# Attention: the order in which SyncE issues the second inverse sums and the next loads

## The chip, the cores and the metric

The kernel runs on one core of one Trainium2 chip. The metric is the device time of one execution in microseconds, given as a median of several runs. TensorE (PE) multiplies, VectorE (DVE) and ScalarE (ACT) do the elementwise work, GpSimd (POOL) adds masks here, and SyncE (SP) issues nearly all DMAs, in the order of its own program.

## What is computed

One layer of a decoder for 1024 tokens of width 1024: RMSNorm, one input projection, an RG-LRU branch and an attention branch of 8 heads (head size 128), gates, an output projection, and a mixture of 32 experts. Only the attention branch matters here:

```python
c = jnp.cumsum(log_f, axis=1).transpose(0, 2, 1)
for qb in range(S // Q_BLOCK):               # 8 query blocks of 128
    s = jnp.einsum('bqhd,bkhd->bhqk', q[:, lo:hi], k[:, :hi]) * scale
    s = s + c[:, :, lo:hi, None] - c[:, :, None, :hi]
    s = jnp.where(causal, s, -jnp.inf)
    p = jax.nn.softmax(s, axis=-1)
    outs.append(jnp.einsum('bhqk,bkhd->bqhd', p.astype(v.dtype), v[:, :hi]))
```

## The kernel before

The kernel is a row of stages with a barrier of all engines between them; attention is the sixth of nine. Every float32 product is made from three products of high and low parts.

**A head in the attention stage.** The stage takes the heads h0 to h7 one after another (`i` is the pair, `c` the head in it, so head 2i + c). Of each head it takes the query blocks 7 down to 0, and a tile is one query block with all of its keys, so the tiles get shorter: tile 0 has 1024 keys, tile 7 has 128. All engines run the same list of steps, one tile each: `scores` of tile n on PE (L1097), `bias` and minimum on DVE (L1186, which writes `least`), the exponential with its row sum on ACT (L1146), the reciprocal of the sum on DVE (L1183, into `inv`, two steps later), the transposes back (`turn`, L1106), the split in high and low (L1140, L1161), three steps later. The products with the values (`values`, L1121) come in two groups of four tiles, the first (g = 1, tiles 0 to 3) seven steps after tile 3 and the second (g = 0, tiles 4 to 7) seven steps after tile 7, so in steps 2 and 6 of the next head. Behind each group DVE multiplies the result by the inverse sums: `output`, L1170, which writes `at_o`. It waits for the PE product and for the inverse sums of this half.

**The way of the inverse sums.** `inv` holds them along partitions, and `at_o` needs them along the free axis, the same in all partitions. So SyncE writes 2 KB of them to DRAM (L1032, "the write"), waits until that has landed, and reads them back to all 128 partitions (L1035, 256 KB, "the broadcast"). This is `inverses(i, c, g)`. The first half can be written when tile 3 has its reciprocal, the second half when tile 7 has its own.

**What SyncE does for a head.** `head(i, c)` issues in this order: the first half's write, the wait for its landing and its broadcast; the store of the previous head's second half (L1027, 256 KB); the values of the next head (L951, two DMAs of 512 KB; they wait for the previous head's products); the queries and keys (L946, 2048 KB) and the bias (L947, 512 KB) of the head after the next, which wait until the last tile of this head has its scores; the second half's write, the wait for its landing, its broadcast; the store of this head's first half. All these DMAs are on one queue. The head buffers are double (`c`), and so are `inv_b` and `o_sb` (by half). The last two heads load no queries and keys, and the last no values.

Of the kernel before, what the change touches and what calls it, by code (L numbers as in the profile page):

```python
# [90 lines left out]
class Kernel:  # L91
# [721 lines left out]
    def branch_out(self, branch):  # L813

        nc, k_ = self.nc, self
# [25 lines left out]
        with nc.Block() as block:  # L841
            @block.sync
            def _(sp):
                if branch == 0:
                    for s, c in both:
                        sp.wait_ge(k_.sig_stored[s][c], 16 * (D // WB))
                else:
                    for k in range(4, KD):
                        for g in range(2):
                            sp.wait_ge(k_.o_stored[g], 16 * (k + 1))  # L850
                        sp.wait_ge(in_lo, k - 3)
                        sp.dma_start(stage[k % 4][:, :], k_.o_d[k]).then_inc(in_loaded[k % 4], 16)

                def gates(i):
                    for s, c in both:
                        sp.wait_ge(gated[s][c], i)
                        sp.dma_start(sg[s][c][:, :], k_.sig_d[branch, 4 * i + 2 * s + c]).then_inc(loaded[s][c], 16)
                with sp.Fori(0, n_pairs - 1) as i:
                    gates(i)
                    for s in range(2):  # L860
                        k_.load_block(sp, s, p0 + i + 1, k_.w_block(weights, WB * (2 + s) + 2 * WB * i))
                gates(n_pairs - 1)
                if branch == 0:

                    for c in range(2):
                        sp.wait_ge(k_.qk_stored[c], 16 * NH)
                        sp.wait_ge(k_.v_stored[c], 16 * NH // 2)
                    sp.wait_ge(k_.bias_stored, 16)
                    for c in range(2):
                        if c == 0:  # L870
                            k_.load_head_qk(sp, 0, c)
                        k_.load_head_v(sp, 0, c)
                for s in range(2):
                    k_.load_block(sp, s, p0 + n_pairs, k_.w_block(following, WB * s))

            @block.tensor
            def _(pe):
                with pe.Fori(0, n_pairs) as i:
                    for s, c in both:
                        if c == 0:  # L880
                            pe.wait_ge(k_.w_lo[s], p0 + i + 1)
                        pe.wait_ge(gated[s][c], i)
                        k_.product(pe, k_.ps[2 * s + c], s, c, in_lo if (s, c) == (0, 0) else None).then_inc((k_.w_first, k_.w_used)[c][s], 1)

            @block.scalar
            def _(act):
                for k in range(KD):
                    if branch == 1:
                        act.wait_ge(in_loaded[k % 4], 16 * (k // 4 + 1))
                    act.activation(k_.uh[:, k, :], source(k), ACT.Copy).then_inc(in_hi, 1)  # L890
                def mixed_high(i, s, c):
                    if branch == 1 and (i, s, c) != (n_pairs - 1, 1, 1):
                        n = 4 * i + 2 * s + c
                        act.wait_ge(gated[s][c], i + 1)
                        act.activation(k_.mix_h[:, n, :], k_.mix[:, n, :], ACT.Copy).then_inc(mix_hi, 1)
                for i in range(n_pairs):
                    k_.split_hi(act, 1, p0 + i)
                    for c in range(2):
                        mixed_high(i, 0, c)
                    k_.split_hi(act, 0, p0 + i + 1)  # L900
                    for c in range(2):
                        mixed_high(i, 1, c)

            @block.vector
            def _(dve):
                for k in range(KD):
                    dve.wait_ge(in_hi, k + 1)
                    dve.tensor_tensor(k_.ul[:, k, :], source(k), k_.uh[:, k, :].bitcast(F32),  # L908
                                      ALU.subtract).then_inc(in_lo, 1)
                def mixed_low(i, s, c):  # L910
                    if branch == 1 and (i, s, c) != (n_pairs - 1, 1, 1):
                        n = 4 * i + 2 * s + c
                        dve.wait_ge(mix_hi, n + 1)
                        dve.tensor_tensor(k_.mix_l[:, n, :], k_.mix[:, n, :], k_.mix_h[:, n, :].bitcast(F32),
                                          ALU.subtract).then_inc(mix_lo, 1)
                for i in range(n_pairs):
                    k_.split_lo(dve, 1, p0 + i)
                    for s, c in both:
                        dve.wait_ge((k_.w_first, k_.w_used)[c][s], p0 + i + 1)
                        dve.wait_ge(loaded[s][c], 16 * (i + 1))  # L920
                        mix = k_.mix[:, bass.ds(4 * i + 2 * s + c, 1), :].rearrange("p a t -> p (a t)")
                        if branch == 0:
                            dve.tensor_tensor(mix, k_.ps[2 * s + c][:, :], sg[s][c][:, :], ALU.mult)\
                                .then_inc(gated[s][c], 1)
                        else:
                            dve.tensor_tensor(sg[s][c][:, :], k_.ps[2 * s + c][:, :], sg[s][c][:, :], ALU.mult)\
                                .then_inc(own, 1)
                            dve.wait_ge(own, 4 * i + 2 * s + c + 1)
                            dve.tensor_tensor(mix, mix, sg[s][c][:, :], ALU.add).then_inc(gated[s][c], 1)
                        mixed_low(i, s, c)  # L930
                        if (s, c) == (0, 1):
                            k_.split_lo(dve, 0, p0 + i + 1)
# [11 lines left out]

    def load_head_qk(self, eng, i, c):
        eng.dma_start(self.at_qk[c][:, :, :].bitcast(F32), self.qk_d[2 * i + c]).then_inc(self.qk_in[c], 16)  # L946
        eng.dma_start(self.at_bias[c][:, :], self.bias_d[2 * i + c].partition_broadcast(P)).then_inc(self.bias_in[c], 16)  # L947

    def load_head_v(self, eng, i, c):
# [4 lines left out]
    def attention(self):  # L954
# [4 lines left out]
        nc, k_ = self.nc, self  # L959
# [49 lines left out]
        def later(engine, semaphore, count):  # L1009

            if type(count) is not int or count > 0:
                engine.wait_ge(semaphore, count)

        with nc.Block() as block:
            @block.sync
            def _(sp):
                def load_qk(i, c):
                    sp.wait_ge(least, tiles * i - tiles + NT * (c + 1))
                    k_.load_head_qk(sp, i, c)

                def load_v(i, c):
                    sp.wait_ge(pv_mm, 4 * i - 2 + 2 * c)
                    k_.load_head_v(sp, i, c)

                def store(i, c, g):
                    sp.wait_ge(o_out, 4 * i + 2 * c + 2 - g)
                    sp.dma_start(k_.o_d[2 * i + c][:, g * HALF:(g + 1) * HALF], o_sb[g][:, :]).then_inc(stored[g], 16)  # L1027

                def inverses(i, c, g):
                    sp.wait_ge(inverted, tiles * i + NT * c + 8 - 4 * g)  # L1030
                    rows = k_.inv_d[4 * i + 2 * c + g]
                    sp.dma_start(rows, inv[c][:, 4 * g:4 * g + 4]).then_inc(inv_stored[g], 16)  # L1032
                    sp.wait_ge(inv_stored[g], 16 * (2 * i + c + 1))
                    later(sp, o_out, 4 * i + 2 * c - g)
                    sp.dma_start(inv_b[g][:, :], rows.rearrange("p b -> (p b)").partition_broadcast(P)).then_inc(inv_in[g], 16)  # L1035

                def head(i, c, first=False, last=False):
                    inverses(i, c, 1)
                    if not first:
                        j, d = (i, 0) if c else (i - 1, 1)  # L1040
                        store(j, d, 0)
                        if not last or d == 1:
                            load_v(j + 1, d)
                    if not last:
                        load_qk(i + 1, c)
                    inverses(i, c, 0)
                    store(i, c, 1)

                k_.load_head_qk(sp, 0, 1)
                head(0, 0, first=True)  # L1050
                head(0, 1)
                for i in range(1, turns - 1):
                    for c in range(2):
                        head(i, c)
# [1075 lines left out]
```

## Time and profile before

| | us |
|---|---|
| median of 3 runs | 1828.74 |
| lowest and highest | 1824.96 and 1829.16 |
| the profiled execution, its own time | 1828.22 |
| its span, from the first to the last instruction | 1826.5 |
| PE busy in the span | 1703.8 (93%) |
| DVE busy | 1037.0 (57%) |
| ACT busy | 840.3 (46%) |

The span starts at 0; attention runs from about 801 to 968 us. In a timeline a line is: start, duration, engine, line, operation, out<-in with the tile's shape, count, and in brackets the idle time of the engine before it and what ended it. "SPq" is SyncE issuing; the duration there is the time of issuing, not of the transfer. Where a line "waited" for several things, the one that came last is named.

### The profile page before, as it was taken

To read this page: it belongs to the slowest core of one execution; us is meant where nothing else is said; L and a number is where in the kernel's file an instruction comes from. 1 tells how busy PE (TensorE), PEld (TensorE's weight loads), DVE (VectorE), ACT (ScalarE), POOL (GpSimd) and SP (SyncE) were. 2 spreads that over 40 slices of the span, in tenths; PEclk is the share of its full clock that TensorE was granted. 3 is DMA by queue.
4 is the path that set the end of the run, shared out by engine and by line. 5 is a ranking of instruction groups with operands and counts; after the bars stand their busy time and mean duration, and the time that the engine had idled before them with its cause. 6 is when DMAs were issued, how large, how long until landed. Compare 5 with 4: busy or idle time off the path is not lost. (4 is left out here: it accounts for less than half of the span.)

```text
span 1826.5 us, 22589 instructions
## 1 busy us (share of the span) xinstructions
PE 1703.8 (93%) x8515; PEld 1364.1 (75%) x8515; DVE 1037.0 (57%) x1125; ACT 840.3 (46%) x845; POOL 137.6 (8%) x187
## 2 busy tenths in 40 slices
PE   5999999999999998999888999969999999999991
PEld 4888888889987887878777888846667777777760
DVE  4353444432213313247665433769988888888886
ACT  5433334241122212036553111247777777878772
POOL 1000000000000000011110000110000000000005
PEclk9999999999999999999999999979999999999995
DMA  4343333323331223546655240379999999999977
GB/s 151 93 153 95 109 96 131 115 100 111 134 132 63 92 93 137 183 154 230 212 170 180 92 166 36 121 285 391 399 390 398 392 398 392 392 399 392 398 293 280
DMA packets 151686, 390.36 MB, mean 214 GB/s; under 512 B 14009, under 2 KB 73481, under 8 KB 147537
## 3 DMA queue, kind: packets, MB, share of 16 engines
q1 hardware_dynamic: 138368, 343.20, 51.0%
q0 software_dynamic: 8384, 29.63, 5.1%
q10 hardware_dynamic: 4880, 16.82, 2.3%
q8 instruction: 34, 0.56, 0.1%
q14 instruction: 20, 0.16, 0.0%
HBM read 322.15 MB, written 67.46 MB: 213 GB/s over the span
## 5 line engine op out<-in xcount | busy, mean ns | idle before, releaser
L1608 DVE TENSOR_TENSOR e_l<-e_raw,e_h 128x2048 fp32r<-128x2048 f32 x192 | 439.2, 2290 | 64.8 <-ACT e_h L1602 64.5
L1602 ACT ACTIVATE e_h<-e_raw 128x2048 fp32r<-128x2048 f32 x192 | 367.8, 1917 | 84.9 <-PE ps L1637 50.2
L199 PE MATMUL ps<-uh,w_h 128*128 128x512 f32 x1008 | 312.9, 392 | 11.9 <-DVE ul L908 9.7
L199 PE MATMUL ps<-ul,w_h 128*128 128x512 f32 x1008 | 312.1, 391 | 0.0
L199 PE MATMUL ps<-uh,w_l 128*128 128x512 f32 x1008 | 311.7, 391 | 0.0
L183 DVE TENSOR_TENSOR w_l<-w_raw,w_h 128x2048 fp32r<-128x2048 f32 x38 | 87.1, 2292 | 328.5 <-ACT w_h L179 328.5
L199 PEld LDWEIGHTS ps<-uh,w_h 128*128 128x128 f32 x1008 | 189.8, 189 | 52.8 <-issue 13.2
L199 PEld LDWEIGHTS ps<-ul,w_h 128*128 128x128 f32 x1008 | 190.2, 189 | 39.8
L199 PEld LDWEIGHTS ps<-uh,w_l 128*128 128x128 f32 x1008 | 190.2, 189 | 39.7
L1624 PE MATMUL ps<-e_h,e_xth 128*96 128x512 f32 x512 | 205.1, 401 | 6.3 <-DVE e_l L1608 3.0
L1624 PE MATMUL ps<-e_h,e_xtl 128*96 128x512 f32 x512 | 202.6, 396 | 0.0
L1624 PE MATMUL ps<-e_l,e_xth 128*96 128x512 f32 x512 | 201.9, 394 | 0.0
L179 ACT ACTIVATE w_h<-w_raw 128x2048 fp32r<-128x2048 f32 x38 | 72.7, 1914 | 167.6 <-DMA w_raw<-w_in 82.6
L1624 PEld LDWEIGHTS ps<-e_h,e_xth 128*96 128x96 f32 x512 | 83.0, 162 | 46.4 <-issue 7.3
L1624 PEld LDWEIGHTS ps<-e_h,e_xtl 128*96 128x96 f32 x512 | 83.1, 162 | 36.0
L1624 PEld LDWEIGHTS ps<-e_l,e_xth 128*96 128x96 f32 x512 | 83.4, 163 | 31.9
L1637 PE MATMUL ps<-e_h,e_hth 128*96 128x512 f32 x256 | 82.6, 404 | 2.1 <-DVE e_htl L1758 2.1
L1637 PE MATMUL ps<-e_l,e_hth 128*96 128x512 f32 x256 | 80.3, 395 | 0.0
L1637 PE MATMUL ps<-e_h,e_htl 128*96 128x512 f32 x256 | 80.2, 394 | 0.0
L1689 POOL DMA_INDIRECT e_xg<-xn_d,slots_i x30 | 41.3, 1378 | 474.2 <-PE ps L1700 474.2
L211 PE MATMUL ps<-w_h,uh 128*128 128x256 f32 x256 | 72.6, 284 | 0.9 <-PEq L164 0.9
L1097 PE MATMUL ps<-at_qk 128*128 128x512 f32 (+3 forms) x288 | 71.2, 378 | 2.3 <-PEq L164 2.0
(285 smaller groups left out, 2375.3 us busy)
## 6 DMA issues: line engine op xcount, KB each, us to landing
e_raw<-w_exp_gate SPq DMA_DIRECT2D x64, 1024.0 KB, 20.2
e_raw<-w_exp_up SPq DMA_DIRECT2D x64, 1024.0 KB, 20.1
e_raw<-w_exp_down SPq DMA_DIRECT2D x64, 1024.0 KB, 19.5
w_raw<-w_in SPq DMA_DIRECT2D x28, 1024.0 KB, 5.6
qk_d<-qk SPq DMA_DIRECT2D x16, 1024.0 KB, 4.2
at_qk<-qk_d SPq DMA_DIRECT2D x8, 2048.0 KB, 11.6
y_d<-e_y ACTq DMA_DIRECT2D x32, 384.0 KB, 6.5
y_d<-zeros POOLq DMA_DIRECT2D x22, 384.0 KB, 4.2
```

The lines of the kernel that those rows point to most:

```text
L179: act.activation(self.w_h[s][:, :, :], self.w_raw[s][:, :, :], ACT.Copy).then_inc(self.w_hi[s], 1)
L183: dve.tensor_tensor(self.w_l[s][:, :, :], self.w_raw[s][:, :, :], self.w_h[s][:, :, :].bitcast(F32), ALU.subtract).then_inc(self.w_lo[s], 1)
L199: mm = pe.matmul(ps[:, h * HALF:(h + 1) * HALF], w[:, k, :], u[:, k, h * HALF:(h + 1) * HALF], start=first, stop=last)
L211: mm = pe.matmul(ps, u[:, k, rows], w[s][:, k, :], start=first, stop=last)
L1097: mm = pe.matmul(k_.ps[n % 2][:, at:end], q, qk[c][:, part, at:end], start=first, stop=last)
L1602: act.activation(self.e_h[m % SPLIT][:, :, :], self.e_raw[slot][:, :, :], ACT.Copy).then_inc(self.e_hi[m % SPLIT], 1)
L1608: dve.tensor_tensor(self.e_l[slot][:, :, :], self.e_raw[slot][:, :, :], self.e_h[m % SPLIT][:, :, :].bitcast(F32), ALU.subtract).then_inc( ...
L1624: mm = pe.matmul(ps, x[:, k, :], w[:, k, :], start=first and first_piece, stop=last and last_piece)
L1637: mm = pe.matmul(ps[:, c * HALF:(c + 1) * HALF], x[:, at, :], w[:, 2 * k + c, :], start=first, stop=last)
L1689: pool.indirect_dma_start(out=xg[b][:, :], out_offset=None, in_=k_.xn_d, in_offset=bass.IndirectOffsetOnAxis(ap=slots, axis=0)).then_inc(g ...
```

## The change

In a head, SyncE now issues the queries and keys of the head after the next, then does the second half's inverse sums (write, wait, broadcast), and only then issues that head's bias and the next head's values. The bias is split off `load_head_qk` into a function of its own; the two other callers call both, one behind the other, as before. The waits stay with their functions: `load_v` still waits for the products of the head whose buffer it fills.

```diff
@@ branch_out @@
                         if c == 0:
                             k_.load_head_qk(sp, 0, c)
+                            k_.load_head_bias(sp, 0, c)
                         k_.load_head_v(sp, 0, c)
@@ load_head_qk @@
     def load_head_qk(self, eng, i, c):
         eng.dma_start(self.at_qk[c][:, :, :].bitcast(F32), self.qk_d[2 * i + c]).then_inc(self.qk_in[c], 16)
+
+    def load_head_bias(self, eng, i, c):
         eng.dma_start(self.at_bias[c][:, :], self.bias_d[2 * i + c].partition_broadcast(P)).then_inc(self.bias_in[c], 16)
@@ attention, head(i, c) @@
                     if not first:
                         j, d = (i, 0) if c else (i - 1, 1)
                         store(j, d, 0)
-                        if not last or d == 1:
-                            load_v(j + 1, d)
                     if not last:
                         load_qk(i + 1, c)
                     inverses(i, c, 0)
+                    if not last:
+                        k_.load_head_bias(sp, i + 1, c)
+                    if not first and (not last or d == 1):
+                        load_v(j + 1, d)
                     store(i, c, 1)
 
                 k_.load_head_qk(sp, 0, 1)
+                k_.load_head_bias(sp, 0, 1)
                 head(0, 0, first=True)
```

## Rows read from the trace of the kernel before

**Rows 1.** The page's first line.

```profile
span 1826.5 us, 22589 instructions
```

**Rows 2.** Waits, 798 to 970 us: who waited for whom; total, times, longest.

```profile
DVE at_o L1170 <- PE ps L1121: 25.5, 11, 3.7
...
DVE at_o L1170 <- DMA at_invb<-inv_d: 19.0, 5, 4.2
```

**Rows 3.** Timeline of DVE in attention: first tile of a head, and `at_o`.

```profile
816.24 1.22 DVE L1186 CUSTOM_DVE_ANT_0 at_s<-ps,at_bias 128x1024 f32<-128x1024 f32 x1
...
833.98 1.21 DVE L1186 CUSTOM_DVE_ANT_0 at_s<-ps,at_bias 128x1024 f32<-128x1024 f32 x1
...
852.01 1.05 DVE L1170 TENSOR_TENSOR at_o<-ps,at_invb 128x512 f32<-128x512 f32 x1 [3.60 <-DMA at_invb<-inv_d]
...
854.71 1.21 DVE L1186 CUSTOM_DVE_ANT_0 at_s<-ps,at_bias 128x1024 f32<-128x1024 f32 x1
...
861.96 1.09 DVE L1170 TENSOR_TENSOR at_o<-ps,at_invb 128x512 f32<-128x512 f32 x1 [2.54 <-PE ps L1121]
...
937.14 1.05 DVE L1170 TENSOR_TENSOR at_o<-ps,at_invb 128x512 f32<-128x512 f32 x1 [3.84 <-DMA at_invb<-inv_d]
...
939.84 1.21 DVE L1186 CUSTOM_DVE_ANT_0 at_s<-ps,at_bias 128x1024 f32<-128x1024 f32 x1
...
966.54 1.05 DVE L1170 TENSOR_TENSOR at_o<-ps,at_invb 128x512 f32<-128x512 f32 x1 [2.33 <-PE ps L1121]
```

**Rows 4.** Timeline of PE just behind the first of those waits.

```profile
853.71 0.55 PE L1106 MATMUL ps<-ident,at_s 128*128 128x128 f32 x3 [2.21 <-DVE at_ptl L1161]
```

**Rows 5.** Timeline of SyncE's queue in attention: what it issues, and when.

```profile
814.32 0.32 SPq L1035 DMA_DIRECT2D at_invb<-inv_d  x1
815.39 0.33 SPq L946 DMA_DIRECT2D at_qk<-qk_d  x1
...
826.30 0.32 SPq L1035 DMA_DIRECT2D at_invb<-inv_d  x1
...
832.39 0.32 SPq L1035 DMA_DIRECT2D at_invb<-inv_d  x1
...
833.23 1.39 SPq L951 DMA_DIRECT2D at_v<-v_d  x2
834.66 2.46 SPq L946 DMA_DIRECT2D at_qk<-qk_d  x1
...
837.64 0.43 SPq L1032 DMA_DIRECT2D inv_d<-at_inv  x1
848.64 0.32 SPq L1035 DMA_DIRECT2D at_invb<-inv_d  x1
...
854.17 0.32 SPq L1035 DMA_DIRECT2D at_invb<-inv_d  x1
...
917.26 0.32 SPq L1035 DMA_DIRECT2D at_invb<-inv_d  x1
...
931.79 0.32 SPq L1035 DMA_DIRECT2D at_invb<-inv_d  x1
...
938.11 0.32 SPq L1035 DMA_DIRECT2D at_invb<-inv_d  x1
...
946.66 0.33 SPq L1035 DMA_DIRECT2D at_invb<-inv_d  x1
```

**Rows 6.** Windows: busy time of the engines, PEclk, DMA share, GB/s.

```profile
905.00:910.00 5.00, 4.64 (x34) 4.00 (x34) 4.81 (x16) 4.67 (x13) 0.92 (x3) 1.00 0.93 388
...
896.00:911.00 15.00, 14.56 (x86) 12.42 (x86) 11.82 (x35) 9.64 (x23) 2.76 (x6) 1.00 0.79 280
911.00:917.00 6.00, 3.67 (x27) 3.05 (x26) 2.30 (x9) 1.74 (x5) 0.86 (x2) 1.00 0.38 88
```

**Rows 7.** From issue to landing: all 16 broadcasts (L1035); the values issued at 938.95.

```profile
DMA to landing us min/median/max: 3.2/3.8/5.5
...
DMA to landing us min/median/max: 5.7/6.3/6.9
```

## The prediction

> **What bounds the kernel now.** The span is 1826.5 us [rows 1], and every stage ends in a barrier, so a stage that is shorter by some us makes the whole shorter by as much; the change touches attention alone. I read first who waits for whom in it. DVE's `at_o` waits in 11 of its 16 cases for PE's product, 25.5 us together, which is the normal turn of a step. In the other 5 it waits for the broadcast of the inverse sums, 19.0 us together, at most 4.2 [rows 2]. DVE stands still there with PE ready: at 852.01 it comes off a wait of 3.60 us, and PE, which runs ahead for a while, then stands for 2.21 us for the low half that DVE owes it [rows 3, 4].
>
> The price of this is read from the starts of the heads on DVE. From h1's first tile (816.24) to h2's (833.98), no `at_o` waited for a broadcast, and the head took 17.74 us. From there to h7's first tile (939.84) it is 105.86 us for five heads, 21.17 each [rows 3]. Five undisturbed heads would take 88.7, so **17.2 us** are the most that lies in this wait (a part of it is lower clock later in the stage).
>
> Then I read why the broadcast is late, on SyncE's queue. I name two moments of head h: F(h), when SyncE issues the broadcast of the first half, and S(h), of the second half. Both are moments at which a write has just been seen to land. F(1) is 832.39, S(1) 848.64, F(2) 854.17, and so on to F(5) 917.26, S(5) 931.79, F(6) 938.11 and S(6) 946.66 [rows 5]. From F to S is the **long stretch**: broadcast, store, values, queries and keys, bias, write, 4098 KB together; 16.25 us in h1 and 14.53 in h5. From S to the next F is the **short stretch**: broadcast, store, write, 514 KB; 5.53 us behind h1. In the long one the write of 2 KB issued at 837.64 is seen landed at 848.64, 11 us later, because it is last in the queue behind 3.5 MB of loads [rows 5]. F(1) to F(6) is 105.72 us, 21.14 a head: SyncE's own chain has DVE's pace. It is a closed ring: SyncE waits for a landing, issues, waits for the next landing, and the loads stand in the same queue as the small writes. So what bounds these five heads is **the sum of all transfers of a head and of two waits for a landing**, not the second half's wait by itself. That is the point the forecast turns on.
>
> **The change part by part.** Removed from each long stretch of h1 to h5: the values (1024 KB) and the bias (512 KB); from that of h0 the bias, and from that of h6 the values. Added to the short stretch behind it: the same. Calls and bytes are the same in all, and no wait is added; the split of the bias from the queries and keys is at no cost, as both are issued in either order by the same engine. The two callers outside `head` keep their order.
>
> *What a long stretch loses (a).* The nearest row is h0's long stretch, which has neither store nor values: from 814.32 to 826.30, 11.98 us. Of these 0.23 are a later issue of queries and keys (1.07 us behind the broadcast, where 0.84 is SyncE's usual distance from broadcast to the next load) [rows 5]. The bias, 512 KB at the 388 GB/s of a full stretch [rows 6], is 1.35 us, and the missing store of 256 KB at the same rate 0.7. So a long stretch of the new order is 11.98 - 0.23 - 1.35 + 0.7 = 11.1 us. The long stretches of now have a mean of (105.72 - 5 x 5.53) / 5 = 15.6. That gives a = 4.5; against h1's own 16.25 it is 5.2. I take 4.8, between them.
>
> *What a short stretch gains (b).* The nearest row is the long stretch of h6, which has no queries, keys and bias: broadcast, store, values and write from 938.11 to 946.66, 8.55 us [rows 5]. Less the short stretch's 5.53, the values cost 3.0, and with 1.35 for the bias b is 4.4. At the mean rate of the stretch that is loading, 280 GB/s [rows 6], the 1536 KB take 5.6, the upper bound. I take 4.8, nearer to the first: the row has the very transfers, and the write there was not last behind a store, which makes it a little short. So a and b are equal, and **the ring stays as long as it is**.
>
> *The waits move.* In the new order S(h) comes 4.8 us sooner against F(h), and the next F is where it was. DVE needs 7.25 us from a head's first tile to the first half's `at_o` (854.71 to 861.96) [rows 3] and was ready for h1's second half at 852.01 - 3.60 = 848.4. S(1) falls from 848.64 to 843.8 and its broadcast lands 3.8 us later [rows 7], at 847.6: the first of the five waits is gone. Then DVE, at 17.74 a head, catches up with the ring of 21.1 again, and the rest of the waits come back smaller, and at the first half's `at_o` too, which now has the long queue ahead of it. The ring's pace is DVE's pace once more, only with DVE further ahead.
>
> *How far ahead at the end.* By S: S(5) = 931.79 - 4.8 = 927.0, landed at 930.8, and h7 begins 2.7 us later (852.01 to 854.71), at 933.5. From h7's first tile to the last `at_o` are 966.54 - 939.84 = 26.7 us [rows 3], which gives 960.2. By the ring: F(6) = 938.1 as before. h6 now has a long stretch without values: S(6) = 938.1 + 5.5 = 943.6. The values of h7 go behind it: F(7) = 943.6 + 8.55 = 952.2. Then S(7) = 952.2 + 5.5 = 957.7, and with 3.8 for the broadcast the last `at_o` starts at 961.5. The ring is later than DVE, so it decides: 961.5 instead of 966.54, **5.0 us less**. In the kernel before, the ring was no bound at this end, since DVE was far behind it. Here it takes back 1.3 us of what DVE has won.
>
> *The values are later.* They are issued behind the broadcast at S + 0.8 and landed up to 6.9 us after issue without a bias ahead [rows 7]; with it, some 8.2, so at S + 9.0. PE needs them about 2.4 us after the next head's first tile (4.6 us of products before the `at_o` at + 7.25), and that tile starts at S + 3.8 + 2.7 = S + 6.5: PE needs them at S + 8.9. That is a tie, and costs nothing as long as `at_o` needs the first half's broadcast, which lands at S + 10.3 + 3.8 = S + 14.1. The bias is needed a whole head later, and is covered.
>
> The Trainium skill's page "DMA: Bandwidth & Descriptors", section "Anatomy of one DMA — SWDGE (gpsimd) path", gives each DMA about 2.0 us fixed, most of it the receipt of the last write, and its bytes at 436 GB/s. By this the long stretch would be some 11.6 us and h6's 5.6; the trace has 15.6 and 8.55, so I don't go by it. By it alone the bytes moved behind the short stretch would partly fall into fixed time that is idle now, which is the first rival.
>
> **The rivals.** *The transfers hide in the short stretch.* From 911 to 917 the DMA engines are busy 0.38 of the time, at 88 GB/s, against 0.79 in the stretch before [rows 6]. 0.62 x 6 = 3.7 us stand idle, and if the bias and the values went into that, b would be 1.1 and not 4.8. Then the ring is 3.7 us shorter a head, 17.4, and DVE's own pace of 17.74 bounds: the waits vanish. Of the 17.2 us I leave some 2 to the lower clock: 15 less, 1813. Against it: h6's stretch, in which the values had the same idle time and still cost 3.0. A half-way case (b = 3.8) gives 5 us more than the forecast, 1818. Chance 0.16.
>
> *The wait only changes its place.* If b is larger than a by 0.8 to 1 us (a = 4.5 and b = 5.4, both inside their rows), each of the five heads loses 0.9, F(6) comes at 942.6, and the gain of 5.0 is used up: 1827.7. For it: in the short stretch the write stands right behind a store to DRAM. Chance 0.14.
>
> *Slower: PE waits for the values.* They were issued 10 us before the second half's broadcast and are issued behind it now. `at_o` of the second half needs the broadcast at S + 10.3 + 10.8 + 3.8 = S + 24.9 at the earliest, and from the values' landing to it are 4.9 + 7.3 = 12.2 us of work. So values that land later than S + 13 make every head longer, us for us. I have them at S + 9.0. SyncE can be held at issuing, too: queries and keys issued behind values took 2.46 us instead of 0.33 [rows 5], and the store and the next write now stand in that place. If they land at S + 15.5, five heads lose 2.5 each, 12.5, less the 5.0: 1836. Against it is the landing of 6.9. Chance 0.06. That the change doesn't do what it says can't be: SyncE issues in the program's order.
>
> **How the numbers follow.** Forecast: 1828.2 - 5.0 = **1823.2**, from the profiled execution's own 1828.22, which is 0.5 under the median of 1828.74. Each 0.5 us of difference between a and b is worth 2.5 us; with a from 4.5 to 5.2 and b from 4.4 to 5.6 the forecast's own range is 1819 to 1829. Chance 0.62; 0.02 is left for what I don't see. 0.3% is 5.5 us, about what a measurement of this kernel tells from no change; the forecast lies just inside it, so I give 0.26 of its 0.62 to faster and 0.36 to the same. Faster: 0.26 + 0.16 = 0.42. Same: 0.36 + 0.14 + 0.02 = 0.52. Slower: 0.06. The range reaches into the first rival: 1815.5 to 1829.2.
>
> **What would show it.** In the changed kernel's timeline of SyncE, from F to S about 11 us (10.4 to 11.1) and from S to the next F about 10.3, and their sum still near 21. If the sum falls below 20, the first rival is right; if it rises over 22, the second. DVE's waits for the broadcast should fall from 19.0 to between 8 and 13 us and be spread over more than five `at_o`, some of the first half. h3's first tile comes at 851.7 and not at 854.71. The last `at_o` starts near 961.5 and waits for its broadcast, and the write-to-landing time of the second half falls from 11 us to some 6. PE must show no long wait for `at_v`. The prediction is wrong if the ring's length depends on the order, that is, if a and b differ by more than 0.5.

## The result, and the profile after

The changed kernel takes 1829.75 us (median of 18 runs, 1826.4 to 1833.04), the kernel before beside it 1826.22 (18 runs, 1823.68 to 1829.16): 1.0016 times as long, 95% interval 1.0008 to 1.0023, so 1.5 to 4.2 us **slower**, where 5.0 us faster was forecast. By the bound of 0.3% it is no change; by its interval it is a small loss. The profiled execution took 1831.69 us.

The page's first line, then the waits from 798 to 975 us (who waited for whom: total, times, longest), answering to [rows 1, 2]:

```profile
span 1830.1 us, 22589 instructions
```

```profile
DVE at_o L1176 <- DMA at_invb<-inv_d: 26.5, 7, 4.6
...
POOL at_bias L1085 <- DMA at_bias<-bias_d: 21.6, 5, 5.8
DVE at_o L1176 <- PE ps L1127: 20.3, 9, 6.1
...
PE ps L1127 <- DMA at_v<-v_d: 1.9, 1, 1.9
```

DVE waits for broadcasts 7 times and not 5, 26.5 us and not 19.0. Where it does, the product of PE has become ready in the same time, so part of these waits was there before under PE's name. PE's wait for the values is small. All waits of `at_o` together are 46.8 us, where they were 44.5.

The timeline of DVE (start, duration, line, tile, and in brackets the idle time before it), answering to [rows 3]:

```profile
816.75 1.22 DVE L1192 CUSTOM_DVE_ANT_0 at_s<-ps,at_bias 128x1024 f32<-128x1024 f32 x1
...
852.23 1.21 DVE L1192 CUSTOM_DVE_ANT_0 at_s<-ps,at_bias 128x1024 f32<-128x1024 f32 x1
...
870.55 1.05 DVE L1176 TENSOR_TENSOR at_o<-ps,at_invb 128x512 f32<-128x512 f32 x1 [3.90 <-DMA at_invb<-inv_d]
...
881.75 1.10 DVE L1176 TENSOR_TENSOR at_o<-ps,at_invb 128x512 f32<-128x512 f32 x1 [3.41 <-DMA at_invb<-inv_d]
...
939.43 1.22 DVE L1192 CUSTOM_DVE_ANT_0 at_s<-ps,at_bias 128x1024 f32<-128x1024 f32 x1
...
968.78 1.05 DVE L1176 TENSOR_TENSOR at_o<-ps,at_invb 128x512 f32<-128x512 f32 x1 [2.31 <-PE ps L1127]
```

From h1's first tile to h3's are 35.48 us, twice 17.74: the first wait has gone, as forecast (36.05 in a second profile of the same kernel). Four heads later h7 begins 122.68 us after h1, where it was 123.60: nearly all of the start has been given back. To the last `at_o` are 152.03 us, against 150.30 before. Waits are now at the first half's `at_o` too (881.75). The 1.7 us between 152.03 and 150.30 are the part of the loss that attention shows in this pair of profiles. Of the 3.5 us between the two spans, 0.5 lie ahead of h1's first tile and 1.3 behind the last `at_o`, where both kernels issue the same in the same order. Two profiles of one and the same kernel differ by up to 2.2 us in these parts, so I can't place them.

The timeline of SyncE's queue, answering to [rows 5]; the broadcasts (L1038) are the moments F and S in turn:

```profile
833.32 0.32 SPq L1038 DMA_DIRECT2D at_invb<-inv_d  x1
833.68 0.44 SPq L1030 DMA_DIRECT2D o_d<-at_o  x1
834.16 0.43 SPq L947 DMA_DIRECT2D at_qk<-qk_d  x1
...
843.67 0.32 SPq L1038 DMA_DIRECT2D at_invb<-inv_d  x1
844.03 0.43 SPq L950 DMA_DIRECT2D at_bias<-bias_d  x1
844.51 1.25 SPq L954 DMA_DIRECT2D at_v<-v_d  x2
845.80 4.64 SPq L1030 DMA_DIRECT2D o_d<-at_o  x1
850.49 0.43 SPq L1035 DMA_DIRECT2D inv_d<-at_inv  x1
855.65 0.32 SPq L1038 DMA_DIRECT2D at_invb<-inv_d  x1
...
944.18 0.32 SPq L1038 DMA_DIRECT2D at_invb<-inv_d  x1
...
948.97 0.32 SPq L1038 DMA_DIRECT2D at_invb<-inv_d  x1
...
958.05 0.32 SPq L1038 DMA_DIRECT2D at_invb<-inv_d  x1
...
963.68 0.32 SPq L1038 DMA_DIRECT2D at_invb<-inv_d  x1
```

F(1) is 833.32, S(1) 843.67, F(2) 855.65, F(6) 944.18. The long stretches of h1 to h5 have a mean of 10.57 us (15.56 before), the short ones 11.61 (5.59 before). The ring F(1) to F(6) is **110.86 us** and was 105.72. So the long stretch lost 5.0 and the short one gained 6.0. The sum of the two, 22.2 us a head, is over the 22 that the prediction named as the sign of its second rival.

Windows of the same profile (busy time and number of instructions of PE, PEld, DVE, ACT, POOL; PEclk; DMA share; GB/s) at two of the waits:

```profile
870.00:872.00 2.00, 0.00 (x0) 0.00 (x0) 1.45 (x2) 0.00 (x0) 0.00 (x0) 0.94 0.97 286
872.00:875.00 3.00, 2.75 (x9) 2.46 (x10) 2.94 (x10) 1.49 (x4) 0.91 (x2) 0.50 1.14 320
...
936.00:938.00 2.00, 0.00 (x0) 0.00 (x0) 1.41 (x2) 0.00 (x0) 0.00 (x0) 1.00 0.87 238
938.00:941.00 3.00, 2.46 (x12) 1.90 (x13) 2.95 (x10) 1.18 (x4) 0.72 (x2) 1.00 1.15 327
```

PE does nothing from 870 to 872, and behind it the granted clock is 0.50, the lower of its two levels. Behind the like pause from 936 to 938 it stays at 1.00. A cost beyond the waits themselves isn't seen: h3 and h4 take 21.03 and 21.66 us from first tile to first tile, and 17.74 with the part of their waits that an undisturbed head doesn't have makes 21.22 and 21.74.

### The profile page after: what moved, and what is told of

Read it like the earlier page. It is cut to its first block and busy times, and to the rows that moved or that the text cites. A ratio compares the mean times of both kernels' runs of the same rounds, so it can differ in the third digit from the quotient of the medians.

```text
span 1830.1 us, 22589 instructions
## 1 busy us (share of the span) xinstructions
PE 1703.5 (93%) x8515; PEld 1362.6 (74%) x8515; DVE 1036.8 (57%) x1125; ACT 841.2 (46%) x845; POOL 138.5 (8%) x187
```

## The experiments

All are read by the same numbers: the means of the five long and the five short stretches of h1 to h5, the ring F(1) to F(6), the time from h1's first tile to the last `at_o`, and the ratio to the kernel before, run beside it, with its 95% interval. All in us but the ratio.

| kernel | long | short | ring | h1 to last `at_o` | median | ratio |
|---|---|---|---|---|---|---|
| before | 15.56 | 5.59 | 105.7 | 150.3 | 1826.22 | |
| before, second profile | 15.60 | 5.46 | 105.3 | 150.6 | | |
| changed | 10.57 | 11.61 | 110.9 | 152.0 | 1829.75 | 1.0016 [1.0008, 1.0023] |
| changed, second profile | 10.38 | 11.74 | 110.6 | 152.0 | | |
| e1, bias alone moved | 14.02 | 7.44 | 107.3 | 149.9 | 1830.84 | 1.0012 [1.0001, 1.0023] |
| e2, values alone moved | 11.83 | 10.07 | 109.5 | 150.8 | 1830.87 | 1.0010 [0.9999, 1.0021] |
| e3, changed, store first | 11.14 | 10.36 | 107.5 | 146.0 | 1827.25 | 0.9996 [0.9988, 1.0005] |
| e4, changed, bias behind values | 10.23 | 11.68 | 109.6 | 155.3 | 1834.08 | 1.0032 [1.0020, 1.0044] |
| e7, changed, values by head | 10.56 | 11.07 | 108.1 | 147.9 | 1824.51 | 0.9978 [0.9967, 0.9989] |
| e8, before, values by head | 14.69 | 5.71 | 102.0 | 143.0 | 1822.07 | 0.9965 [0.9953, 0.9978] |
| e10, before, no store ahead of the write | 15.71 | 4.41 | 100.6 | 141.8 | 1822.77 | 0.9975 [0.9964, 0.9986] |
| e5, loads in the landings | | | 89.2 | 132.8 | 1811.35 | 0.9910 [0.9895, 0.9924] |
| e6, inverse sums on GpSimd | | | | 139.8 | 1819.49 | 0.9949 [0.9936, 0.9963] |
| e9, e5 with values by head | | | 90.2 | 132.9 | 1810.76 | 0.9910 [0.9895, 0.9925] |

The kernel before beside e1 to e4 took 1828.57, beside e5 to e8 1828.25, beside the others 1827.80. The medians are of 4 to 12 runs, that of the changed kernel of 18, those of the kernel before of 16 to 29; each second profile is a single run (1827.12 and 1831.18 us). The stretches and the attention time are those of one profiled execution, which in e1 and e5 was the fastest of its kernel, so they and the medians need not agree to a us or two.

**Is the surplus of the ring real?** The two kernels once more, with no edit.

> The kernel before once more, for a second profile: how much of the differences between stretches is the spread from one execution to the next. If the ring is a property of the order, F(1) to F(6) is 105.7 within 1.5 us, the long stretch 15.6 and the short one 5.6 within 0.3.

> The changed kernel once more, for a second profile. If b is larger than a by a property of the order, F(1) to F(6) is 109 to 112, the short stretch 11.3 to 11.9 and the long one 10.3 to 10.9. If the 5 us between the two rings was chance, it comes out under 108.

Both rings come back within 0.5 us, and all four mean stretches within 0.2. The 5 us between the rings belong to the order and not to chance. In the second profile of the changed kernel the last `at_o` waits for its broadcast, as the forecast had it:

```profile
DVE at_o L1176 <- DMA at_invb<-inv_d: 38.5, 11, 4.8
```

**Which of the two moves makes it?**

```diff
 # e1: only the bias behind the second half's inverse sums
                         store(j, d, 0)
+                        if not last or d == 1:
+                            load_v(j + 1, d)
...
                         k_.load_head_bias(sp, i + 1, c)
-                    if not first and (not last or d == 1):
-                        load_v(j + 1, d)
 # e2: only the values
                         load_qk(i + 1, c)
+                        k_.load_head_bias(sp, i + 1, c)
                     inverses(i, c, 0)
-                    if not last:
-                        k_.load_head_bias(sp, i + 1, c)
```

> The bias alone is moved behind the second half's broadcast; the values stay ahead of queries and keys as in the kernel before. Measure: SyncE's ring from F(1) to F(6), 105.7 us before and 110.9 in the changed kernel, and the time. Theory A (the surplus comes from the values: SyncE is held 4 to 5 us at issuing the store behind them, so the store and the write start late): ring 105 to 107, time as before within 1.5 us. Theory B (the surplus comes from the bias, which is slow right behind the broadcast, both being spread to all partitions from one row of DRAM): ring 109 to 111, time 2 to 4 us above before.

> The values alone are moved behind the second half's broadcast; the bias stays with queries and keys. Theory A (hold at issue behind the values): ring F(1) to F(6) 109 to 111, SyncE's store issue still takes 4 us or more, time 2 to 4 us above before. Theory B (slow bias behind the broadcast): ring 105 to 107, time at or 1 to 4 us under before, because h6's stretch to S is shorter.

Moved alone, the bias takes 1.5 from the long stretch and gives 1.9 to the short one; the values take 3.7 and give 4.5. Both moves lose, 0.3 and 0.8 us a head, together the 1.1 of the change. e1's ring of 107.3 is just outside theory A, and far from theory B; e2's 109.5 is in theory A, but its store is issued in 2.1 to 3.9 us and not in 4 or more. The medians of both are 2.3 us over before though attention is at its old length. e1's interval just excludes no change and e2's doesn't, and the record doesn't say where these 2.3 us lie.

**The order behind the broadcast.**

```diff
 # e3
                     inverses(i, c, 0)
+                    store(i, c, 1)
                     if not last:
                         k_.load_head_bias(sp, i + 1, c)
                     if not first and (not last or d == 1):
                         load_v(j + 1, d)
-                    store(i, c, 1)
 # e4
                     inverses(i, c, 0)
+                    if not first and (not last or d == 1):
+                        load_v(j + 1, d)
                     if not last:
                         k_.load_head_bias(sp, i + 1, c)
-                    if not first and (not last or d == 1):
-                        load_v(j + 1, d)
                     store(i, c, 1)
```

> The changed kernel, but the store of the first half is issued right behind the second half's broadcast, ahead of bias and values. Theory A: the store's own latency is overlapped again, but the next write is now the one held behind the values; ring 107 to 110, so up to 0.7 us a head less than the 110.9 of the changed kernel. Theory B: with the store between broadcast and bias the bias is not slowed, ring 105 to 107.

> The changed kernel, but with the values ahead of the bias behind the second half's broadcast. Bytes and queue are the same. Theory A: SyncE is now held at issuing the bias, and the store and the write after it are late as before; ring 110 to 112. Theory B: the bias is no longer beside the broadcast, ring 106 to 107.5 and the time within 1.5 us of before.

e4 has the short stretch of the changed kernel, 11.68, and a ring of 109.6, just under theory A and far over theory B's 107.5: taking the bias away from beside the broadcast does not make the stretch shorter, and theory B falls. e4 shows something else on DVE's timeline, in front of h3's first tile:

```profile
855.09 0.16 DVE L1189 RECIPROCAL at_inv<-at_small 128x1 f32<-128x1 f32 x1 [2.45 <-POOL at_bias L1085]
855.17 1.22 DVE L1192 CUSTOM_DVE_ANT_0 at_s<-ps,at_bias 128x1024 f32<-128x1024 f32 x1
```

The head waits for its mask, and the mask for the bias: the bias of h3 is issued at S(1), in the middle of h2, and is needed 8.6 us later, not "a whole head later", as the prediction said; for h4 to h7 it is 7.0 to 7.5 us. In the changed kernel it has landed 6.3 to 6.7 us behind S, just in time (POOL waits 21.6 us for it; DVE's waits for POOL are 4.3 us together, as before). Behind the values it lands 9.4 to 11.8 us behind S, DVE waits 18.6 us for POOL, and attention is 3.3 us longer than in the changed kernel.

e3 is 1.25 shorter in the short stretch than the changed kernel and 0.6 longer in the long one; attention is 4.3 us shorter than before. Its median is not clear of before (0.9996, interval 0.9988 to 1.0005). The ring of 107.5 fits theory A in size, but the next two show that the hold is not the reason.

**Is SyncE held at issuing?** The store behind the values took 4.64 us to issue. A layout of the values in DRAM head by head makes runs of 4 KB out of runs of 512 bytes:

```diff
-        self.v_d = dram("v_d", (NH // 2, 2, P, NT, WB))
+        self.v_d = dram("v_d", (NH // 2, 2, P, 2, NT, HD))
...
-                          self.v_d[i, part, :, :, c * HD:(c + 1) * HD]).then_inc(self.v_in[c], 16)
+                          self.v_d[i, part, :, c, :, :]).then_inc(self.v_in[c], 16)
```

with the staging tiles of the stage that writes them in the same form.

> The changed kernel, with the values kept in DRAM head by head, so that a head's values are 2 x 128 runs of 4 KB instead of 2 x 1024 runs of 512 bytes. Theory A (SyncE is held at issuing behind the 2048 small runs, and store and write start late): the issue of the store behind the values falls from 4.2 us to under 1.5, the short stretch from 11.6 to 8.5 to 10 us, the ring F(1) to F(6) from 110.9 to 95 to 103, and the time by 4 to 12 us against the changed kernel. Rival (the bytes cost as much in either form): ring 108 or more.

> The kernel before, with the same head-by-head layout of the values in DRAM. Theory A: the issue of queries and keys behind the values falls from 2.5 to 0.5 us, the long stretch loses 1 to 2 us (15.6 to about 14), the ring falls from 105.7 to 97 to 102, time 4 to 8 us under before. Rival (bytes alone count): ring 104 to 106, time as before.

SyncE's queue in e7:

```profile
866.96 0.32 SPq L1038 DMA_DIRECT2D at_invb<-inv_d  x1
867.32 0.43 SPq L950 DMA_DIRECT2D at_bias<-bias_d  x1
867.80 1.03 SPq L954 DMA_DIRECT2D at_v<-v_d  x2
868.88 0.98 SPq L1030 DMA_DIRECT2D o_d<-at_o  x1
869.90 0.78 SPq L1035 DMA_DIRECT2D inv_d<-at_inv  x1
878.20 0.32 SPq L1038 DMA_DIRECT2D at_invb<-inv_d  x1
```

The hold is gone, 0.98 us where the same head of the changed kernel has 4.18, and the write is issued 2.9 us behind the broadcast where it was 6.4. But it is seen landed only 8.3 us later, where it was 4.2, and the short stretch has lost 0.54 in the mean. The layout takes 0.5 us off the stretch that has the values in the changed order and 0.9 off it in the order before; the surplus of the order stays: with this layout the short stretch gains 5.4 where the long one loses 4.1. So theory A of e7, that the hold makes the surplus, has fallen: its ring of 108.1 is in the rival's range. Its time is 5 us under the changed kernel, as theory A had it, but the layout gives as much in the old order. There, in e8, the numbers came as its theory A had them (ring 102.0, 6.2 us under before), but for the long stretch, which lost 0.9 and not 1 to 2. By the two ratios the layout is worth 6 to 7 us in either order.

**What does a store ahead of the write cost?**

```diff
                     if not first:
                         j, d = (i, 0) if c else (i - 1, 1)
+                        store(j, d, 1)
                         store(j, d, 0)
...
                     inverses(i, c, 0)
-                    store(i, c, 1)
+                    if last and c == 1:
+                        store(i, c, 1)
```

> The kernel before, with the store of a head's first half issued one long stretch later, so that nothing but the broadcast stands ahead of the next write. Theory receipt (a write that stands right behind a 256 KB store to DRAM is seen landed about 1 us later, beside the 0.7 us of the store's bytes): the short stretch falls from 5.6 to 3.8 to 4.2, the long one grows by 0.6 to 0.8, the ring F(1) to F(6) falls from 105.7 to 99 to 102, time 3 to 6 us under before. Rival (bytes alone count, so what the short stretch loses the long one gains): ring 105 to 106.5, time as before.

SyncE's queue there:

```profile
868.05 0.32 SPq L1035 DMA_DIRECT2D at_invb<-inv_d  x1
868.41 0.43 SPq L1032 DMA_DIRECT2D inv_d<-at_inv  x1
873.18 0.32 SPq L1035 DMA_DIRECT2D at_invb<-inv_d  x1
873.54 0.91 SPq L1027 DMA_DIRECT2D o_d<-at_o  x2
```

The short stretch falls from 5.5 to 4.4 in the mean (3.2 to 5.6 in the five heads; this one is one of the longer), and the long one grows by 0.1 only. So a 256 KB store right ahead of the small write costs 1.1 to 1.2 us, and in the middle of the long stretch next to nothing. This is what e3 has gained, 1.25. The theory had 0.7 us for the bytes in either place, and a short stretch of 4.2 at most; that was wrong, and the rest of it held: ring 100.6, attention 8.5 us shorter, the time 1.4 to 3.6 per mille less.

**Is the ring the bound?** The same transfers, with loads issued while a write is landing:

```diff
-                    inverses(i, c, 1)
+                    inverses_out(i, c, 1)
                     if not first:
                         j, d = (i, 0) if c else (i - 1, 1)
+                        if not last or d == 1:
+                            load_v(j + 1, d)
+                    inverses_in(i, c, 1)
+                    if not first:
                         store(j, d, 0)
                     if not last:
                         load_qk(i + 1, c)
-                    inverses(i, c, 0)
+                    inverses_out(i, c, 0)
                     if not last:
                         k_.load_head_bias(sp, i + 1, c)
-                    if not first and (not last or d == 1):
-                        load_v(j + 1, d)
+                    inverses_in(i, c, 0)
                     store(i, c, 1)
```

`inverses_out` is the first half of `inverses`, the write; `inverses_in` the wait for its landing and the broadcast.

> All transfers as in the changed kernel, but SyncE issues a load while each of its two writes is still landing: the next head's values between the first half's write and its broadcast, the bias between the second half's write and its broadcast. Theory ring (SyncE's chain of transfers and two waits for a landing is the pace of heads h1 to h6): the idle time of the landings, some 2 x 2.5 us a head, is filled, F(1) to F(6) falls from 105.7 to 85 to 92 us, that is to DVE's and PE's own 17.74 a head, DVE's waits for the broadcast nearly vanish, and the time falls by 10 to 15 us against before. Rival (the waits are set by the bytes ahead of a broadcast alone): F(1) to F(6) stays over 103, the time within 3 us of before.

SyncE's queue, and DVE's waits:

```profile
864.18 0.32 SPq L1034 DMA_DIRECT2D inv_d<-at_inv  x1
866.36 1.24 SPq L954 DMA_DIRECT2D at_v<-v_d  x2
867.71 2.67 SPq L1040 DMA_DIRECT2D at_invb<-inv_d  x1
```

```profile
DVE at_o L1181 <- PE ps L1132: 24.9, 14, 3.3
DVE at_o L1181 <- DMA at_invb<-inv_d: 1.4, 2, 0.8
```

The write lands while SyncE waits for the values' buffer and issues the values. The broadcast, behind the values, takes 5.2 to 6.9 us here instead of 4.0 in the mean, and DVE hardly waits for it, since it starts so much sooner. The ring is 89.2 us, 17.84 a head, DVE's and PE's own pace. Attention is 17.5 us shorter and the kernel 16.9, a ratio of 0.991, more than the 10 to 15 us of theory ring. This is the gain that was there to take, 17.2 by [rows 3], and with e9 the best of the kernels run. With the values by head on top there is no more to get:

> The kernel with the loads issued in the landings, with the values kept head by head as well. Theory ring: that kernel is already at DVE's and PE's own 17.8 a head and waited only 1.4 us for broadcasts, so cheaper values give no more than those 1.4 us: 1809 to 1812, as without the layout. Rival (the layout is worth 3 to 6 us by itself, as it was on both other orders, 1824.5 against 1828 to 1830 and 1822.1 against 1828.3): 1804 to 1808.

As the theory said: 1810.76 and 1811.35, both 0.9910 of the kernel before beside them.

**Another queue.** From the kernel before, GpSimd issues writes and broadcasts, each broadcast one mask behind its write.

```diff
+                for h in range(NH):
+                    for m in range(NT):
+                        diagonal(h // 2, NT * (h % 2) + m)
+                        if m == 2 and h > 0:
+                            inverses_out(h - 1, 0)
+                        if m == 3 and h > 0:
+                            inverses_in(h - 1, 0)
+                        if m == 6:
+                            inverses_out(h, 1)
+                        if m == 7:
+                            inverses_in(h, 1)
```

> From the kernel before: the writes and broadcasts of the inverse sums are issued by GpSimd on its own queue, the write one mask ahead of the broadcast; SyncE has only loads and stores, in the order of the kernel before. Theory ring: nothing of SyncE's loads is in the chain any more, heads take 17.7 to 18.2 us on DVE, the waits for the broadcast vanish, 12 to 16 us less than before. Rival (the 16 DMA engines are shared, so the small write is behind 3.5 MB on any queue): the write still lands 8 to 10 us after its issue and most of the 19 us of waits stay.

Between the two expectations: attention 10.5 us shorter, the kernel 8.8. The waits for broadcasts fall to 8.4 us, but a head takes some 19 us and not 17.8. GpSimd's timeline shows why:

```profile
866.85 0.57 POOL L1078 DMA_DIRECT2D at_invb<-inv_d  x1 [5.46 <-DMA inv_d<-at_inv]
867.44 0.47 POOL L1070 TENSOR_TENSOR at_bias<-at_bias,at_mask 128x128 f32<-128x128 f32 x1
```

Its write, issued at 859.65 on another queue while queries and keys are loading, is seen landed at 866.85 all the same, 7.2 us later, and the mask behind the wait is late: DVE waits 10.6 us for masks in this kernel and 4.3 before.

## Why the prediction was wrong

**Right.** What bounds: the ring of SyncE's transfers and landings, as e5 shows by breaking it for 16.9 us and leaving every transfer in. The gain at hand, 17.2. That the bytes moved do not hide in the short stretch (the first rival): they cost it more than their price. That the first wait goes (h3's first tile at + 35.48 us from h1's, forecast 35.5), that waits come back at both halves, and that PE's wait for the values is no bound (1.9 us), which was the third rival. The values land 9.7 to 11.3 us behind S, forecast 9.0, and were to hurt from 13 on. a was forecast at 4.8 and is 5.0 to 5.2; that is luck in part, since its row gave 4.5 with a new long stretch of 11.1 (measured 10.4 to 10.6), and the rest came from averaging with h1's single 16.25. The tail's sum holds as well: with the measured F(6) of the two profiles, 944.2 and 946.2, it gives 967.6 and 969.6 for the last `at_o`, which starts at 968.8 and 970.5. The forecast had 145.26 us from h1's first tile to the last `at_o`, and the measured 152.03 is 6.8 more: 5.1 from the ring, 0.4 from a later F(1) and 1.2 behind F(6).

**The step that failed is b**, what the short stretch gains: forecast 4.8, measured 6.0 and 6.3, both over the 5.6 that the prediction called the upper bound. The ring doesn't stay as long as it is: the difference of 1.0 between b and a is 5.1 us in five heads, just the gain forecast. This is the second rival, which had been given 0.14 and 1827.7. b was put together from two rows that don't fit each other. The values were priced as h6's long stretch less a short one, 8.55 - 5.53 = 3.0 [rows 5]. But the short stretch has a store right ahead of its write and h6's stretch does not, and e10 shows that this place costs 1.1 to 1.2: the base should have been some 4.4, the values 4.1.

The trace of the kernel before can settle the price without a difference of stretches. In h6's stretch the store issued at 938.47 has landed 4.2 us later, at 942.7 (the one DMA of L1027 in that place, from issue to landing):

```profile
DMA to landing us min/median/max: 4.2/4.2/4.2
```

and the second half of the values, issued at 939.52, has landed 6.9 us later [rows 7], at 946.4. So the values took 3.8 us and not 3.0. The same reading for all stretches of h1 to h5: each step is the time from one landing to the next, in the order of the queue (the broadcast from its issue), in the mean of five.

| step, us | long, before | short, before | long, changed | short, changed |
|---|---|---|---|---|
| broadcast | 4.0 | 3.8 | 4.1 | 4.4 |
| store | 0.7 | 1.6 | 0.7 | 1.3 |
| values | 3.6 | | | 3.6 |
| queries and keys | 5.7 | | 5.5 | |
| bias | 1.3 | | | 2.1 |
| write, to the next broadcast's issue | 0.3 | 0.2 | 0.2 | 0.2 |

So b is 3.6 for the values, 2.1 for the bias, 0.6 for a broadcast that lands later, less 0.3 for the store. The forecast had 3.0, 1.35 and nothing for the broadcast, 4.4 together, and put 0.4 on top. The prediction named the store's place as a reason for "a little short", and gave it no price.

What makes b larger than a is to be seen there too. The values' own step is the same in both places (3.6; 3.7 and 3.5 in the second pair of profiles). The bias takes 0.8 more right behind the broadcast than behind the queries and keys, and the broadcast 0.6 more with loads behind it; the second pair has 0.8 and 0.5. The first half's broadcast, which had loads behind it all along, has 4.0 in both profiles before and 4.1 and 4.4 in the changed kernel. The second half's is at 4.2 with the bias alone behind it (e1), at 4.8 with the values (e2), and at 5.0 in e4, where the bias, now behind the values, takes 1.5: broadcast and bias together take 6.4 and 6.5 in the two orders. So the surplus goes with the head of a short stretch that has loads queued in it, and not with one of the loads. Why these first transfers take longer there stays open; it is not the hold at issuing (e7).

**A second miss**, without effect on the time: the waits for broadcasts were forecast at 8 to 13 us and came to 26.5, since a wait that a broadcast ends takes in the 2.5 us for PE that were there anyhow. The second half's write was to be seen landed in some 6 us and takes 7.1 to 9.9, since it is issued sooner. And the bias was said to be covered by a head, while it has 7 to 9 us; e4 shows what happens when they are used up. The 2 us that the first rival left to the lower clock were not lost either: in e5 every head from h1 on takes 17.7 to 17.9 us.

## What to carry to other kernels

When an engine issues a small write, waits for its landing and issues the next thing, all on the queue that carries the loads, the loop of landings and bytes is a ring, and in this kernel its length was what counted (e5). Here a change of the order within it moved a wait from one consumer to the other and made the ring longer. What shortened it was to issue a load while the landing is awaited (0.9% of the kernel), and to keep a store to DRAM from standing right ahead of the small write. And where a transfer's price is taken as the difference of two stretches, both must end in the same way; the landings of the transfers within one stretch give the price without that trap.

## What the hardware showed that I had not expected

- A 256 KB store to DRAM right ahead of a 2 KB write on the same queue delayed the sight of its landing by 1.1 to 1.2 us; moved among the loads, it cost 0.1 (e10). By the landings, the store takes 1.6 us there and 0.7 with loads behind it.
- Issuing a DMA behind two loads of 1024 runs of 512 bytes each held SyncE for up to 4.64 us, 5.09 in the second profile; with runs of 4 KB for 0.98. The time until the data had landed hardly changed (short stretch 11.61 and 11.07).
- A 2 KB write on GpSimd's queue took 7.2 us to be seen landed while SyncE's queue was loading 16 KB runs: a queue of its own did not spare it the loads. The writes that it issued between the loads took 1.7 to 2.8 us.
- Behind 2 us without PE work (870 to 872) the granted clock was 0.50 for the next 3 us; behind another 2 us (936 to 938) it was 1.00.
